# Carried rows of a bidirectional state-space scan: accumulated in TensorE, or transposed into a bank of their own and added by VectorE

## The reference, cut to what matters

```python
cb = jnp.einsum("bclgn,bcsgn->bclsg", cc, bc)
y_diag = jnp.einsum("bclsgr,bcsgrp->bclgrp", cb[..., None] * decay, xdt)
y_off = jnp.einsum("bclgn,bcgrpn->bclgrp", cc, h_enter) * jnp.exp(a_cum)[..., None]
return (y_diag + y_off), h_last        # forward and backward are added
# after it: y = (y + d_skip * xs) * silu(z), a norm per group, and the output product
```

## Time and profile before

| | us |
|---|---|
| median of 3 runs | 1197.61 (1197.46 to 1197.94) |
| profiled execution, its own time | 1197.97 |
| its span, first to last instruction | 1196.2 |
| PE busy in the span | 1160.4 (97%) |
| DVE busy | 840.1 (70%) |
| ACT busy | 616.8 (52%) |

### The profile page before, as it was taken

How to read it: one execution, slowest core, us unless ns; L and a number is a source line. 1 busy time by engine, 2 the same in 40 slices (tenths; PEclk the granted TensorE clock), 3 DMA queues, 4 the chain that set the end, 5 groups by cost and what they waited for, 6 DMA issues and landing times.

```text
span 1196.2 us, 17207 instructions
## 1 busy us (share of the span) xinstructions
PE 1160.4 (97%) x6430; PEld 931.2 (78%) x6430; DVE 840.1 (70%) x1208; ACT 616.8 (52%) x1074; POOL 84.4 (7%) x73
## 2 busy tenths in 40 slices
PE   5999999999999999999999999999999899999998
PEld 3667677787777787887887887887887579998997
DVE  4563677887978656893882882897777977754655
ACT  5541484848574546621421421446854777654553
POOL 0000101010010043000000000044000004000000
PEclk9999999999999999999999999999999999999999
DMA  9856543332322233643633633632333005455554
GB/s 362 343 182 218 194 126 108 106 124 80 123 80 80 88 114 103 244 142 126 230 138 128 232 131 132 231 129 71 124 133 132 2 2 176 159 186 184 191 180 156
DMA packets 49893, 179.13 MB, mean 150 GB/s; under 512 B 5216, under 2 KB 7584, under 8 KB 47776
## 3 DMA queue, kind: packets, MB, share of 16 engines
q1 hardware_dynamic: 49536, 177.66, 43.5%
q10 hardware_dynamic: 288, 0.56, 0.1%
HBM read 177.05 MB, written 1.15 MB: 149 GB/s over the span
## 4 chain that ended last, share of the span: by engine, by line
PE 80%; DVE 8%; ACT 7%; DMA 2%; issue 2%; SPq 0%; DVEq 0%; ACTq 0%
PE ps L1929 51%; PE ps L1936 9%; PE ps L2223 6%; ACT ey L1268 3%; PE ps L2021 2%; PE ps L1952 2%; DVE sm L1877 1%; ACT ey L1271 1%; DMA mhalf<-in_w_mod 1%; DVE prob L1902 1%; PE ps L2134 1%; DVE ycomb L1709 1%; PE ps L2341 1%; DMA xload<-in_ctx 1%; ACT mixF L1255 1%
## 5 line engine op out<-in xcount | busy, mean ns | idle before, releaser
L1412 DVE TENSOR_TENSOR w_lo<-raw,w_hi 128x1024 fp32r<-128x1024 f32 x206 | 261.9, 1272 | 89.1 <-ACT w_hi L1042 89.0
L1042 ACT ACTIVATE w_hi<-raw 128x1024 fp32r<-128x1024 f32 x206 | 216.7, 1053 | 191.3 <-DMA raw<-in_w_ff 154.6
L1929 PE MATMUL ps<-a_hi,w_hi 128*128 128x512 f32 (+1 forms) x820 | 299.2, 365 | 0.0
L1929 PE MATMUL ps<-a_hi,w_lo 128*128 128x512 f32 (+1 forms) x820 | 288.9, 352 | 0.0
L1929 PE MATMUL ps<-a_lo,w_hi 128*128 128x512 f32 (+1 forms) x820 | 288.7, 352 | 0.0
L1929 PEld LDWEIGHTS ps<-a_hi,w_hi 128*128 128x128 f32 x820 | 155.1, 189 | 25.1 <-issue 2.7
L1929 PEld LDWEIGHTS ps<-a_lo,w_hi 128*128 128x128 f32 x820 | 155.1, 189 | 23.2 <-issue 1.0
L1929 PEld LDWEIGHTS ps<-a_hi,w_lo 128*128 128x128 f32 x820 | 155.0, 189 | 21.3
L1929 PE MATMUL ps<-b_hi,w_hi 128*128 128x512 f32 x304 | 119.2, 392 | 0.0
L1929 PE MATMUL ps<-b_lo,w_hi 128*128 128x512 f32 x304 | 118.5, 390 | 0.0
L1929 PE MATMUL ps<-b_hi,w_lo 128*128 128x512 f32 x304 | 118.3, 389 | 0.0
(11 more groups left out here) (289 smaller groups left out, 1762.0 us busy)
## 6 DMA issues: line engine op xcount, KB each, us to landing
raw<-in_w_ff SPq DMA_DIRECT2D x128, 512.0 KB, 3.5
mring<-in_w_mod SPq DMA_DIRECT2D x32, 768.0 KB, 5.2
raw<-in_w_in_even SPq DMA_DIRECT2D x36, 512.0 KB, 5.5
mring<-in_w_mod SPq DMA_DIRECT2D x16, 1024.0 KB, 5.1
ey<-acum_rows SPq DMA_DIRECT2D x32, 384.0 KB, 5.1
raw<-in_w_in_odd SPq DMA_DIRECT2D x18, 512.0 KB, 3.5
mhalf<-in_w_mod SPq DMA_DIRECT2D x16, 512.0 KB, 9.7
raw<-in_w_out_even SPq DMA_DIRECT2D x16, 512.0 KB, 3.5
```

What stands on the lines that cost most here:

```text
L1042: nc.scalar.activation(w_hi[:, u % RING, :, :], raw[:, u % RING, :, :], ACT.Copy).then_inc(hi_done, 1)
L1412: v.tensor_tensor(w_lo[:, u % RING, :, :], raw[:, u % RING, :, :], w_hi[:, u % RING, :, :].bitcast(F32), ALU.subtract).then_inc(lo_done, 1)
L1929: ins = mm(out_ap, w_[:, n % RING, k, :], (x_[k][:, 0:ntok] if type(x_) is list else x_[:, k, 0:ntok]), start=(k == 0 and j == 0), stop=(k ...
```

## The change

The identity matmuls leave the step `y` and become a step `yx` of their own: three transposes of `ycomb` into bank 7 (`B_AUX[1]`), one chunk later, right behind the products of the next `yoff`. The step `yt` on DVE gets a second addition, from bank 7. In the list `yoff` moves ahead of `seg` of the next chunk (ahead of `yt` as well), and `yx`, `yt` follow it. DVE's `yoff` waits for the last `yx` in place of the last `y`, because both touch `ycomb`.

```diff
         for n in range(NCH):
+            s.append(("yoff", g, ch[n]))
+            if n:
+                s += [("yx", g, ch[n - 1]), ("yt", g, ch[n - 1])]
             if n < NCH - 1 and not last:
                 s.append(("seg", g, "f", ch[n + 1]))
-            if n:
-                s.append(("yt", g, ch[n - 1]))
-            s.append(("yoff", g, ch[n]))
             mixsplits(0, *((), (2, 3), (6, 7), ())[n])
...
-        s.append(("yt", g, ch[-1]))
+        s += [("yx", g, ch[-1]), ("yt", g, ch[-1])]
         slot(6)
...
+        elif k == "yx":
+            job(st, B_AUX[1])
...
-                        dve.wait_ge(*filled(("y",) + yo_l[n - 1][1:]))
+                        dve.wait_ge(*filled(("yx",) + yo_l[n - 1][1:]))
...
                     part = mixF[:, FN_T + XT * g:FN_T + XT * g + XT, P * ch:P * ch + P]
+                    v.tensor_tensor(part, part, ps[:, b, 0:GX].rearrange("p (i l) -> p i l", i=XT), ALU.add).then_inc(freeing(key), 1)
+                    key = ("yx", g, ch)
+                    b = jobs[key][0]
+                    dve.wait_ge(*filled(key))
+                    dve.wait_ge(*latest())
                     v.tensor_tensor(part, part, ps[:, b, 0:GX].rearrange("p (i l) -> p i l", i=XT), ALU.add).then_inc(freeing(key), 1)
...
-                                mm(..., start=(i == 0 and di == 0), stop=False, skip_group_check=True)
+                                ins = mm(..., start=(i == 0 and di == 0), stop=(di == 1), skip_group_check=True)
+                    ins.then_inc(filling(st), 1)
+                elif k == "yx":
+                    n = y_n[("y",) + st[1:]]
                     pe.wait_ge(y_done, n + 1)
+                    b = jobs[st][0]
+                    if free_before[st]:
+                        pe.wait_ge(*emptied(st))
                     for i in range(XT):
-                        ins = mm(ps[:, b, P * i:P * i + P], ycomb[:, n % 2, P * i:P * i + P], ident, start=False, stop=True, skip_group_check=True)
+                        ins = nc.tensor.transpose(ps[:, b, P * i:P * i + P], ycomb[:, n % 2, P * i:P * i + P], ident)
                     ins.then_inc(filling(st), 1)
```

## The result

| | before | after |
|---|---|---|
| median, same chip | 1197.94 us (1197.46 to 1198.38, 5 runs) | 1204.68 us (1202.50 to 1205.12, 5 runs) |
| ratio, 95% interval | | 1.0049 [1.0037, 1.0061] |
| profiled execution, its own time | 1197.97 | 1203.59 |
| its span | 1196.2 | 1201.8 |

The change makes the kernel slower by 0.49%, 6.7 us by the medians and 5.6 us by the two profiled executions. The forecast was 1198.8 with a range up to 1203.0; the measured median lies outside it. A second measurement of the same changed kernel, shown further down, gave 1204.21. The profiled execution is 1.1 us under the median of after; what follows explains its 5.6 us, and the 1.1 lies within the spread of the five runs.

What follows compares the result with a forecast made beforehand. PE and DVE were taken as nearly level, DVE's lateness deciding: +0.1 us for the groups before group 3 and +1.05 in group 3 gave +1.15, so 1198.8 against the median; own range 1196.5 to 1201, wider range 1193.5 to 1203.

Steps and rivals of the forecast that it cites:

- what bounds: In the scan PE and DVE run nearly level; relieving one helps only until the other is late.
- new wait at `toks`: Before the `toks` transposes PE would wait about 3 us for DVE, three times.
- PE's part: Per chunk in the scan PE saves 0.45 us, 7.2 over 16 chunks, and 5.1 us of waits go too.
- Bank 7 is free by then: When `yx` transposes into bank 7, the bank has already been released; no wait was priced.
- 0.63 between waited additions: On DVE each `yt`'s two additions take 0.63 us each, so a `yt` costs 1.26 where it cost 0.46.
- rival of longer steps: In the scan every waited DVE start takes 0.67: 0.8 us in a group, 0.4 in group 3; 1201.6 us, 19%.
- terms up to the sixth split tile: In group 3, two `yt` and the scalings ahead of that tile make DVE's chain 1.49 us late.
- way from the split tile to the next product: In group 3, lateness goes from +1.49 us at the sixth split tile to +1.05 at the next product.
- From there PE has no wait in which this could be made up: Behind the scan, from the next product on, the 1.05 us lateness of group 3 stays.
- The clock: Rival: the 3.1 us stall before `toks` lowers the clock three times, up to 1.9 us each; 1204.5 us, 10%.
- DVE no limit: Rival: in the scan PE keeps its 3.1 us in each of three groups; 1189.5 us, 6%.
- DVE cheaper: Rival: DVE's added or changed spacings in the scan cost 0.46 us each, 1.36 off a group; 1194.6 us, 15%.

Runs made afterwards that it cites:

- two banks: The changed kernel with the carried rows in banks 3 and 7 in turn, so that no `yx` waits for an addition; 1205.27 us.
- other bank for the last chunk: The changed kernel with only the sixteenth `yx`, the last of group 3, going to bank 3 instead of bank 7; 1203.07 us.
- kernel with doubled additions: The kernel before with each of DVE's 16 `yt` additions made twice, PE's work and the order untouched; 1205.67 us.
- delayed PE: The kernel before with 17 spare, overwritten matmuls on PE ahead of the third output product, making PE 3.9 us late behind the scan; 1201.86 us.
- fastest kernel: The kernel before with the new order in groups 0 to 2 and, in group 3, two split tiles ahead of additions and next scaling; 1192.92 us.
- filled one: The changed kernel with carried rows in banks 3 and 7 in turn, plus three spare matmuls on PE ahead of the wait at `toks`; 1202.15 us.

## Why the prediction was wrong, point by point

**Right: what bounds.** "The two engines run nearly level, and what one is relieved of helps only until the other is late." Six kernels bear it out: 16 more additions on DVE cost 7.8 or 7.9 us with either PE work, and PE's waits move about without the time following them. The new wait at `toks`, DVE without a gap over 0.23 us to the fifth `silu`, the short transposes (387.52 to 387.80, 0.28, where 0.33 was put) and the wait for the split tile all stand where they were forecast. Their sizes were smaller: 1.6 us at `toks` instead of 3, because the bank took its part, and 2.2 at the split tile instead of over 3, because PE had by then waited 1.7 us more at three places of group 3. PE's part was near: it was to stand still for 3.1 us before `toks`, and with two banks it does for 2.8, with DVE 0.3 later than forecast. A chunk frees 0.34 us of PE and not 0.45, but that shortfall cost nothing in groups 0 to 2, where PE stood waiting for DVE anyway.

**The failed step: "Bank 7 is free by then."** This was looked at for the first three `yx` of a group, where 4 us lie between, and not for the fourth, which stands one decay product behind the third. There the second addition of the chunk before has barely been issued. The prediction's own pieces say so: in group 3 its scaled rows are ready at 384.56, the second addition behind them starts at 384.56 + 0.63 = 385.19 and lasts 0.55, so the bank is free at 385.7 and not at 384.56. In group 3 it costs 1.12 us (1.18 with the 0.06 above), shown by the other bank for the last chunk. In groups 0 to 2 it costs nothing: with two banks, and so without it, `toks` of group 1 start at 189.36, in the changed kernel's second profile at 189.28:

```profile
189.28 0.55 PE L2151 MATMUL ps<-c,xbc 128*128 128x128 f32 x3 [1.63 <-DVE xbc L1637]
```

**The failed size: 0.63 between waited additions.** They start 0.65 and 0.66 apart, so that a `yt` costs 1.31 to 1.32 instead of 1.26. That is 0.22 of the 0.31 us by which the chain of group 1 is longer than forecast (35.49 against 35.18). Most of the rest lies between a decay product and the `silu` behind it, 1.07 to 1.10 where 1.04 was put. In the kernel with doubled additions, where one wait stands between the two, they start 0.58 apart; the change puts two waits there (for its own bank and for the addition before), and it is 0.65. That the second wait makes the difference is read from the code; no run varies it alone. The slack of 0.33 before `toks` was the whole cushion: a group that should have cost 0.04 cost 0.4 to 0.55, the scan entered group 3 at +1.3 and not at +0.1. The rival of longer steps had this mechanism, at 0.67, and put 0.8 us on a group; its 1201.6 was nearer than the forecast.

**Group 3.** The terms up to the sixth split tile were right: 1.51 for the two `yt` and scalings against 1.49. A gap of 0.47 us came on top at the norm's products, 0.35 of it new:

```profile
358.64 2.07 DVE L1746 SCALAR_TENSOR_TENSOR mixF<-mixF,vec,gate 128x512 f32<-128x512 f32 x3 [0.47 <-DVE gate L1423]
```

No experiment looked at it. The way from the split tile to the next product was forecast as -0.44 (from +1.49 to +1.05) and is -0.40 without the bank. The scan's account by the rows: 1.3 entering, 0.35 the gap, 1.5 the two `yt`, -0.4, 1.2 the bank, together +3.95. The forecast had 0.1, 0, 1.49, -0.44, 0. With the 1.8 behind the scan, at which it put nothing either, that is the whole miss in the profiled execution: 1.2 for the chain of the groups, 0.35, 1.2 and 1.8 over a forecast of +1.15.

**Behind the scan.** "From there PE has no wait in which this could be made up" was right, but that anything could be added was not thought of. 1.8 us were in both profiles. That it isn't the lateness as such is shown by the delayed PE. The rows put most of it on weight loads landing late in layer 1, and 0.3 in one profile on the clock; what makes the loads land late stays open. It isn't special to the change either: the fastest kernel loses 1.2 us behind its scan, and the filled one nothing. No rival held it.

**The clock.** The rival named a mechanism that exists, at the right place, but it didn't come true in the scan in either profile of this kernel. The likely reason is one that the failed step hid: the bank wait splits the stall of 3 us in two. With two banks it came true in two groups of three. Its price of 1.9 each was above the 1.5 found there. That the measured 1204.68 lies next to this rival's 1204.5 is chance: the time was lost elsewhere.

**DVE no limit, and DVE cheaper.** Both are refuted: at `toks` PE waited 4.9 us in all, and the two additions of a `yt` never started less than 0.65 apart, where the cheap case needed 0.46.

**What was missed altogether** is that the change's own new order is its good half. The working priced it inside the sum (the scaling that falls into DVE's wait for ACT) and never asked what it gives alone: 3.5 us in the scan, which the second additions (7.9) then cost more than twice over.

## What to carry to other kernels

Where two engines run level, price each edit of a change alone on both: here the order alone gained 0.29%, and moving work from PE (0.34 us a chunk) to DVE (0.65 a chunk) turned it into a loss of 0.49%. When a buffer is handed from job to job, check the pair of uses that stand closest, not the typical one. And look at the granted clock behind a new stall of some microseconds: the same 2.8 us brought no fall in nine cases where they came in two pieces, and a fall of about 1.5 us in two of three where they came in one.

## What the runs showed of the hardware that was not expected

- The granted clock can fall to 1.2 GHz after a single stall of 2.8 us between full products (two of three times), or of 2.2 us (once, in the filled kernel, and not in four other profiles with a wait as long at the same place: two of the changed kernel, two banks, other bank). With three spare matmuls in the stall it stayed at 2.4 GHz at all three `toks` of the one profile.
- Two dependent additions of 128x384 on DVE start 0.58 us apart in the kernel with one wait between them and 0.65 in the one with two. An instruction that waits for nothing starts 0.46 behind such an addition.
- Transposes of 128x128 follow each other at 0.11 us at the full clock, and the first three behind a stall take 0.90 instead of 0.55, by their records, at the low one.
